# Moving key copies, routers, bias products, row halves and an index product in a hybrid decoder step

## The reference

```python
z = rmsnorm(x) @ w_in                       # u | q | k | v, 4 x 512 columns
pool_out = linear(window_mean(u) - u) * pool_scale
o = (softmax(q1 k1) - lam * softmax(q2 k2)) @ v        # 4 heads, prompt; sample reads 512 cached positions
h = x + concat(pool_out, rmsnorm(o) * (1 - lambda_init)) @ w_out
top4 of softmax router over 32 experts; per expert: a = h2 @ w1[e] + b1[e]
act = glu * sigmoid(1.702 * glu) * (lin + 1)           # both clamped at 7
y += gate * (act @ w2[e] + b2[e])
out = rmsnorm(h + y)                        # and the new pool, key and value caches
```

## Time and profile before

| what | value |
|---|---|
| median of three runs | 1559.9 us |
| profiled execution | 1562.38 us, span 1560.6 us |
| TensorE (PE) busy | 1461.7 us, 94% |
| VectorE (DVE) busy | 1206.5 us, 77% |
| ScalarE (ACT) busy | 1010.6 us, 65% |
| GpSimd (POOL) busy | 499.2 us, 32% |
| from HBM | 461.87 MB read, 26.49 MB written |

### The profile page before, as it was taken

One profiled execution on the slowest core, in us unless ns is written; L12 is line 12 of the kernel. 1 busy time (PEld: TensorE's weight loads), 2 busy tenths in 40 slices (PEclk: granted clock), 3 DMA queues, 4 the chain that ended last, 5 costly groups with the idle time before them and its releaser, 6 DMA issues.

```text
span 1560.6 us, 23621 instructions
## 1 busy us (share of the span) xinstructions
PE 1461.7 (94%) x7924; PEld 1242.1 (80%) x7925; DVE 1206.5 (77%) x1051; ACT 1010.6 (65%) x907; POOL 499.2 (32%) x437
## 2 busy tenths in 40 slices
PE   6999679878899999999999999999999999999993
PEld 6998358876688888888888888888888888888872
DVE  4313873266698998999898889998999888989992
ACT  4423662244477777777777777777777777777772
POOL 1100000013443334333444443334333444433310
PEclk9999789978899999999999999999999999999996
DMA  8433216527799999999999999999999999999975
GB/s 238 128 110 110 81 51 240 206 101 296 274 354 370 369 367 376 369 367 372 372 379 375 377 378 375 365 368 376 369 362 370 386 371 384 373 375 369 361 281 155
DMA packets 94256, 479.84 MB, mean 307 GB/s; under 512 B 12730, under 2 KB 25546, under 8 KB 44993
## 3 DMA queue, kind: packets, MB, share of 16 engines
q1 hardware_dynamic: 81689, 443.10, 73.7%
q0 software_dynamic: 12528, 36.22, 8.9%
HBM read 461.87 MB, written 26.49 MB: 313 GB/s over the span
## 4 chain that ended last, share of the span: by engine, by line
PE 86%; DVE 6%; DMA 3%; ACT 2%; issue 1%; SPq 1%; POOL 0%; POOLq 0%; DVEq 0%; ACTq 0%
PE ps L1728 66%; PE ps L1436 9%; PE ps L1707 4%; PE ps L1733 2%; DVE lo L1017 2%; PE ps L1701 1%; PE ps L1562 1%; DVE arena L1112 1%; ACT hi L681 1%; DMA arena<-h_rows,idx 1%; DVE stats L1116 1%; PE ps L1612 1%; DMA h_rows<-raw 1%; DMA raw<-cache_v 1%; DMA raw<-w_in 1%
## 5 line engine op out<-in xcount | busy, mean ns | idle before, releaser
L1017 DVE TENSOR_TENSOR lo<-raw,hi 128x2048 fp32r<-128x2048 f32 x268 | 612.4, 2295 | 152.9 <-ACT hi L681 150.8
L681 ACT ACTIVATE hi<-raw 128x2048 fp32r<-128x2048 f32 x268 | 508.9, 1914 | 98.7 <-PE ps L1728 90.9
L1728 PE MATMUL ps<-hi,t_hi 128*128 128x512 f32 x1536 | 442.6, 397 | 11.4 <-DVE lo L1017 3.4
L1728 PE MATMUL ps<-lo,t_hi 128*128 128x512 f32 x1536 | 435.7, 392 | 0.0
L1728 PE MATMUL ps<-hi,t_lo 128*128 128x512 f32 x1536 | 433.8, 391 | 0.0
L1728 PEld LDWEIGHTS ps<-lo,t_hi 128*128 128x128 f32 x1536 | 291.2, 190 | 62.4
L1728 PEld LDWEIGHTS ps<-hi,t_hi 128*128 128x128 f32 x1536 | 285.6, 190 | 68.3 <-issue 8.0
L1728 PEld LDWEIGHTS ps<-hi,t_lo 128*128 128x128 f32 x1536 | 290.1, 189 | 60.7
L1017 DVE TENSOR_TENSOR lo<-arena,hi 128x2048 fp32r<-128x2048 f32 x128 | 293.1, 2290 | 36.2 <-ACT hi L681 36.1
L681 ACT ACTIVATE hi<-arena 128x2048 fp32r<-128x2048 f32 x128 | 245.5, 1918 | 50.4 <-PE ps L1728 50.4
L606 POOL TENSOR_SCALAR t_hi<-cst,rank_c 128x128 fp32r<-128x128 f32 x165 | 216.7, 1327 | 0.0
(11 more groups left out here) (237 smaller groups left out, 1223.8 us busy)
## 6 DMA issues: line engine op xcount, KB each, us to landing
raw<-w SPq DMA_DIRECT2D x256, 1024.0 KB, 7.5
arena<-w SPq DMA_DIRECT2D x128, 1024.0 KB, 8.0
raw<-w_in SPq DMA_DIRECT2D x8, 1024.0 KB, 7.5
raw<-cache_k SPq DMA_DIRECT2D x32, 256.0 KB, 4.9
raw<-cache_v SPq DMA_DIRECT2D x32, 256.0 KB, 5.6
raw<-w_out SPq DMA_DIRECT2D x4, 1024.0 KB, 4.9
raw<-x_prompt SPq DMA_DIRECT2D x4, 512.0 KB, 3.8
arena<-x_prompt POOLq DMA_DIRECT2D x4, 512.0 KB, 5.6
```

Of the source, the lines that this page charges most:

```text
L681: act_e.activation(hi[:, slot, :], raw_at(slot_raw), ACT.Copy).then_inc(s_hi, 1)
L1017: v.tensor_tensor(lo[:, slot, :], raw_at(slot_raw), hi[:, slot, :].bitcast(F32), ALU.subtract).then_inc(s_lo, 1)
L1728: last = pe.matmul(ps[:, base_bank + b, :], lhs[l][:, row, :], r[:, ck.slot(j), at:at + 512], start=first_k and kk == 0 and q == 0, stop=l ...
```

## The change

Nothing that is computed changes. One small activation is added and the others change place in their engine's order:

- `k_out(0)` and `k_out(1)` move ahead of `pro_lo(8)` and `pro_lo(10)` on VectorE.
- On VectorE `norm2(2)` moves behind `o_lo(5)`, `choose(0)` and a residual, `norm2(3)` behind `choose(1)`; on TensorE the quarter products of tile 4 and the transposes change places; on ScalarE `gate_exp` moves ahead of `h2_out`.
- All five `w2_bias` products are made before the first w1 chunk. On VectorE the fourth addition and `rows_lo(0)` come before the `lo` of chunk 1.
- `rows_hi(1)` and `rows_lo(1)` move from between chunks 6 and 7 to behind `head` chunk 0.
- In `body(0)` alone, `index_product(3)` moves from before chunk 2 to before chunk 4, and `indices(3)` from behind `lo` 4 to behind `lo` 5.
- A one-column root on ScalarE is put ahead of the final norm's wait.

```diff
@@ -883,15 +883,15 @@
             h2_out(1)
             o_hi(5)
             gate_exp(0)
+            gate_exp(1)
             h2_out(2)
-            gate_exp(1)
+            gate_exp(2)
             h2_out(3)
-            gate_exp(2)
             act_e.activation(st[:, 60:61], eps, ACT.Sqrt)
             norm2_sums(4)
             act_e.activation(st[:, 61:62], eps, ACT.Exp)
+            gate_exp(3)
             h2_out(4)
-            gate_exp(3)
             gate_exp(4)
 
             def expert_hi(ck, j):
@@ -940,11 +940,11 @@
             act_e.activation(st[:, 62:63], eps, ACT.Gelu_apprx_sigmoid)
             for j in range(RING, W1C):
                 expert_hi(start, j)
-                if j == 6:
-                    rows_hi(1, s_xt, s_xh, x_hi)
             head = Chunks(PRO + W1C, 0)
-            for j in range(3):
-                expert_hi(head, j)
+            expert_hi(head, 0)
+            rows_hi(1, s_xt, s_xh, x_hi)
+            expert_hi(head, 1)
+            expert_hi(head, 2)
             gated(0, 0, W1C)
             gated(0, 1, W1C)
             expert_hi(head, 3)
@@ -993,6 +993,7 @@
 
             further_blocks(act_e, further)
 
+            act_e.activation(st[:, 58:59], eps, ACT.Sqrt)
             for p, t in enumerate(FINAL):
                 n = TILES[t][1]
                 act_e.wait_ge(s_fy[t], 16)
@@ -1066,11 +1067,13 @@
                     last = v.tensor_copy(k_t[:, 2 * hp + hh, 512:544], ps[:, 2 * hh + 1, 0:32])
                 last.then_inc(s_kte, 1)
 
-            for g in range(RING + 1, 10):
+            for g in range(RING + 1, 8):
                 pro_lo(g)
             k_out(0)
+            pro_lo(8)
+            pro_lo(9)
+            k_out(1)
             pro_lo(10)
-            k_out(1)
             pro_lo(11)
 
             for g in range(4):
@@ -1265,15 +1268,16 @@
             norm2(1)
             residual(3, (3,))
             o_lo(4)
-            norm2(2)
             o_lo(5)
             choose(0)
             residual(4, (0,))
-            norm2(3)
+            norm2(2)
             choose(1)
             residual(4, (1,))
+            norm2(3)
+            residual(4, (2,))
             choose(2)
-            residual(4, (2, 3))
+            residual(4, (3,))
             norm2(4)
             choose(3)
             choose(4)
@@ -1351,20 +1355,20 @@
             w2_bias(0)
             w2_bias(1)
             w2_bias(2)
+            w2_bias(3)
+            rows_lo(0, s_xh, s_xl, first_lo, first_hi)
             expert_lo(start, 1)
-            rows_lo(0, s_xh, s_xl, first_lo, first_hi)
             expert_lo(start, 2)
             expert_lo(start, 3)
             indices(1, 1, base + 1)
-            w2_bias(3)
             w2_bias(4)
             for j in range(RING, W1C):
                 expert_lo(start, j)
-                if j == 6:
-                    rows_lo(1, s_xh, s_xl, x_lo, x_hi)
             head = Chunks(PRO + W1C, 0)
-            for j in range(3):
-                expert_lo(head, j)
+            expert_lo(head, 0)
+            rows_lo(1, s_xh, s_xl, x_lo, x_hi)
+            expert_lo(head, 1)
+            expert_lo(head, 2)
             gating(0, W1C)
             expert_lo(head, 3)
             indices(2, 2, base + 2)
@@ -1373,7 +1377,7 @@
                 ck = Chunks(PRO + W1C, n)
                 for j in range(j0, W1C - 1):
                     expert_lo(ck, j)
-                    if j == 4:
+                    if j == (5 if isinstance(n, int) else 4):
                         indices(n + 3, n + 3, n + (base + 3))
                 rows_lo(n, s_ah, s_al, act_lo, act_hi, 4)
                 for j in range(W1C - 1, PER - 1):
@@ -1672,10 +1676,10 @@
             router(0)
             out_product(4, (0,))
             router(1)
+            out_product(4, (1,))
             h2_transposes(2)
-            out_product(4, (1,))
+            out_product(4, (2,))
             router(2)
-            out_product(4, (2,))
             h2_transposes(3)
             out_product(4, (3,))
             router(3)
@@ -1762,9 +1766,12 @@
             pe.wait_ge(s_gtl, 1)
             for t in range(3):
                 w2_bias(t)
+            pe.wait_ge(s_w2a, 1)
+            w2_bias(3)
             pe.wait_ge(s_ixe, 1)
             x_transposes(0, 1)
-            pe.wait_ge(s_w2a, 3)
+            pe.wait_ge(s_w2a, 4)
+            w2_bias(4)
             start = Chunks(PRO, 0)
             for j in range(W1C):
                 if j == 6:
@@ -1773,17 +1780,12 @@
                 w1(start, j, 0, 1, 1, (first_hi, first_lo))
                 if j == 0:
                     index_product(1)
-                if j == 1:
-                    w2_bias(3)
-                if j == 2:
-                    pe.wait_ge(s_w2a, 4)
-                    w2_bias(4)
             pe.wait_ge(s_w2a, NT)
 
             def body(n):
                 ck = Chunks(PRO + W1C, n)
                 for j in range(W1C):
-                    if j == 2:
+                    if j == (4 if isinstance(n, int) else 2):
                         pe.wait_ge(s_ixe, n + 3)
                         index_product(n + 3)
                     if j == 4:
```

## The result

| kernel | median us | runs | ratio to the kernel before, 95% interval |
|---|---|---|---|
| before | 1561.03 | 4 | |
| changed | 1539.88 | 4 | 0.9869, 0.9848 to 0.989 |
| changed, a later comparison | 1543.75 | 6 | 0.9904, 0.9887 to 0.9922 |

The change is faster, by 21.2 us on the medians of the first comparison, against 28.5 forecast; 1539.9 is 8.5 us above the forecast of 1531.4 and outside the likeliest case's own range (1528 to 1535). It lies 0.1 us inside the whole range of 1527 to 1540; the later comparison's 1543.75 lies outside. The profiled execution took 1541.53 us with a span of 1539.6 us, 21.0 less than before.

What follows compares the result with a forecast made beforehand. The prediction took TensorE to bound the kernel, with gains only before the loop or in the tail: 5.8 + 7.7 + 13.8 + 1.2 = 28.5 us, giving a median of 1531.4 us, whole range 1527 to 1540.

Steps and rivals of the forecast that it cites:

- Key copies: Second key transposes: TensorE's 3.2 us wait goes and products behind run faster; 5.8 us saved, bounds 3.2 and 6.0.
- rival C: Key products and tile 4: the clock doesn't come back, 5.4 us stay lost, 1536.8 us; chance 0.08.
- Norms, routers: Tile 4 to the expert count: TensorE starts tile 4 right behind router(0); 7.7 us saved, bounds 4.9 and 8.2.
- First two experts: First experts up to chunk 4 of body(0): TensorE's pauses shrink; 13.8 us saved, bounds 8 and 15.5.
- rival B: One-hot matrix before body(0)'s index product: VectorE splits hold GpSimd, 4.1 us more, 1535.5 us; chance 0.15.
- Rival D: First experts: a chunk or gather lands 5 to 8 us late under full DMA share, 1536.4 to 1539.4; chance 0.07.
- Index product: body(0): moved to chunk 4, else its wait would be paid at chunk 2; part of the 13.8 us.
- Tail: Final norm: the root's table load moves into ScalarE's idle time; 1.2 us saved, bounds 0.3 and 1.3.
- Transfers: First experts, 355 to 385 us: DMA near full share, yet each chunk lands some 4 us or more early.
- rival E: Expert loop: a chunk arrives late in every pass; at 1.2 us each, 36 us lost, 1567 us; chance 0.03.

Runs made afterwards that it cites:

- e6_routing: The kernel before with only the edits of norms, routers, residuals and gate exponentials; 1550.96 us, ratio 0.9951.
- e10_hold4_again: The changed kernel with VectorE waiting before the lo of chunk 4 until expert 1's gather is issued, measured again; 1528.50 us, ratio 0.9801.
- e8: The changed kernel with the bias products and row halves back in their old places; 1539.43 us, ratio 0.9876.
- e4: The changed kernel with the five stores of the sums moved behind the gather for expert 2; 1544.32 us, ratio 0.9908.
- e2: The changed kernel with VectorE waiting before the lo of chunk 4 until GpSimd has issued expert 1's gather; 1529.52 us, ratio 0.9803.
- e3: The changed kernel with VectorE waiting before the lo of chunk 6 until GpSimd has issued expert 1's gather; 1534.38 us, ratio 0.9845.
- e7: The e2 kernel with the index product in body(0) back before chunk 2; 1535.12 us, ratio 0.9849 to the kernel before.
- e1_keys: The kernel before with the key copies alone moved; 1552.97 us, ratio 0.9957.

## Why the prediction was right and wrong

- **Key copies**, 5.8 us: right. The units end at 139.3 instead of 145.0 us, 5.7 us sooner, and alone the edit gave 6.4 (4.5 to 8.9 by the ends of its ratio). The granted clock was 1.00 over these products and over the first quarter product of tile 4 (3.06 us), so rival C didn't come true. For tile 4 it doesn't hold in every execution: of the eleven profiles with the new order two show this product slower, 4.47 us in e6_routing and 4.43 in e10_hold4_again, at a mean granted clock of 0.64.
- **Norms, routers**, 7.7 us: right. 14.1 us at the count less 5.7 are 8.4; alone 7.6. The wait for `cache_v` fell from 1.0 to 0.25 us, which is about the surplus.
- **First two experts**, 13.8 us: wrong. The trace gives 18.3 - 14.1 = 4.2. The step that failed is the sentence that chunks 4 and 5 end at 378.6 and the transposes at 379.6. It took for granted that the gather for expert 1 lands 5 to 6 us after it is issued, as the first two gathers had in the kernel before (6.0 and 5.2). It landed after 19.75, and the transposes started at 371.64 where the forecast, moved by the 14.1 us, has 364.5. That is 7.1 us late. The granted clock was lower in the wait (0.70 from 364 to 368 us), and the transposes and chunk 6 behind it took 5.8 us where the forecast had 3.7: 2.1 us more. These are 9.2 of the 9.6 us by which the term fell short. The edits removed VectorE's pauses, and one of these pauses was what the gather's instruction had been running in (e8). The prediction did name the hold between the two engines, from the earlier trace rows, but put it on the one-hot matrix of expert 3 alone (rival B); the row at 348.79, 2.85 us beside a split, said that a gather is held as well. Rival D, a gather landing 5 to 8 us late, had the right place but not the cause: it put the lateness on the full DMA share, and its 5 to 8 us were too small. e4 rules out the stores, e2 and e3 show what did it.
- What was left of that term held in part. TensorE's waits behind the gather were 1.7 and 2.5 us, as forecast. The matrix of expert 3 ended 9.3 us behind its indices; the prediction has 8.7, though two whole splits in its way would make its own sum 9.8. The start was better than forecast: the first chunk began at 343.95 against 344.8 (358.9 less 14.1) and took 2.86 us instead of 5.46, as the granted clock was 1.00 there and 0.50 in the kernel before. The prediction had kept the old 5.46. TensorE was done with chunk 5 some 3 us sooner than forecast, and in the changed kernel only waited longer for it. With the gather freed this gain shows: in e2_hold4 chunk 4 of `body(0)` starts at 387.83, 30.0 us sooner than before where 27.3 were forecast, and the kernel is at 1528.5 to 1529.5, where the sum had 1531.4. It isn't the forecast kernel, though: it also pays 1.09 us for the hold and 2.62 for the matrix of expert 2, which weren't forecast.
- **Index product**, part of the same term: right. With the gather freed it is worth 5.6 us (e7); in the changed kernel it wasn't tested alone.
- **Tail**, 1.2 us: right, though not tested alone. The load left the chain, 1.29 us. Another 1.1 us came unforeseen and isn't shown to be the change's: the last 48 products took 12.79 instead of 13.90 us, but also 12.80 in e1_keys, which leaves the tail as it was, and 13.93 in e7_hold_index2, which has the tail of the changed kernel. Behind chunk 4 of `body(0)` the span is 2.7 us shorter in all, and 5.7 + 8.4 + 4.2 + 2.7 are the 21.0 us between the two spans.
- **Transfers**: no wait for a weight chunk appeared; the loop passes stayed at 35.93 us, so rival E was wrong.

The Trainium skill ("SBUF — State Buffer", Who interferes with whom) says that VectorE instructions with two SBUF inputs block a GpSimd instruction that reads SBUF, and suggests that writing descriptors isn't blocked by them. The runs agree in part: the five plain stores, which read no index, took 2.72 us in e2_hold4 right beside two splits, the same as in the changed kernel with VectorE idle, while the gather, which reads its index column, was held for 12.19 us. That the index read is what waits was not tested.

## What to carry to other kernels

Before an idle time of one engine is removed, list what other engines do in it; here VectorE's pause was when GpSimd had issued its gather. Where the work of one engine holds an instruction of another, a wait of about 1 us placed on the engine that is ahead can save much more; here it saved ten. When several edits are made together, test each without the others: here the bias products and the row halves earned nothing until the hold on VectorE was added.

## What the runs showed of the hardware

A gather that starts 0.1 us ahead of a row of back-to-back splits doesn't get through between them. Its instruction took 1.12 us alone, 5.58 with two splits, 12.19 and 12.20 with five: each time it ended 1.0 us behind the last split.

A short gap is enough to let it through, and so is another kind of instruction. The changed kernel has both, GpSimd first:

```profile
334.18 3.02 POOL L622 DMA_INDIRECT arena<-h_rows,idx  x1 [2.35 <-issue]
388.37 3.18 POOL L622 DMA_INDIRECT arena<-h_rows,idx  x1 [18.05 <-DVE idx L1302]
```

```profile
333.94 2.27 DVE L1018 TENSOR_TENSOR lo<-raw,hi 128x2048 fp32r<-128x2048 f32 x1
336.14 2.35 DVE L1352 TENSOR_TENSOR arena<-ps,arena 128x1024 f32<-128x1024 f32 x2
...
388.25 2.29 DVE L1018 TENSOR_TENSOR lo<-raw,hi 128x2048 fp32r<-128x2048 f32 x1 [0.78 <-ACT hi L681]
390.97 2.29 DVE L1018 TENSOR_TENSOR lo<-raw,hi 128x2048 fp32r<-128x2048 f32 x1 [0.42 <-ACT hi L681]
```

At 388.37 the gather waited for one split only and ended at 391.55, beside the next one: the 0.42 us between the two splits were enough. At 334.18 the bias additions, which read one operand from PSUM (`ps`), followed the split without a gap, and the gather still ended at 337.20, 1.0 us behind the split. So the hold of 1.09 us in e2_hold4 may be longer than it has to be; a shorter one wasn't tried.
